# Layer 0's border between attention output and feed-forward: one output chunk and one feed-forward chunk by token halves in place of two each

## What is computed

```python
h = h + g1_l * y_l                                  # y_l = o @ w_o
h = h + g2_l * swiglu_ffn(ada_norm(h, norm_ffn[i], sh2_l, sc2_l), ffn_w_in[i], ffn_w_out[i])
# hc, the context, the same with g1_c, sh2_c, sc2_c, g2_c

def rms_norm(x, g):
    y = x * lax.rsqrt(jnp.mean(x * x, axis=-1, keepdims=True) + EPS)
    return y * g

def ada_norm(x, g, shift, scale):
    return rms_norm(x, g) * (1.0 + scale) + shift

def swiglu_ffn(h, w_in, w_out):
    a, g = jnp.split(h @ w_in, 2, axis=-1)
    return (jax.nn.silu(a) * g) @ w_out
```

## Time and profile before

| | us |
|---|---|
| three runs | 1509.53, 1512.20, 1512.33 |
| median | 1512.2 |
| the profiled execution | 1508.97 |
| its span in the trace | 1507.7 |
| PE busy | 1488.3 (99%) |
| DVE busy | 1079.9 (72%) |
| ACT busy | 718.2 (48%) |

### The profile page before, as it was taken

How to read it: one execution, slowest core, us unless ns; L and a number is a source line. 1 busy time by engine, 2 the same in 40 slices (tenths; PEclk the granted TensorE clock), 3 DMA queues, 4 the chain that set the end, 5 groups by cost and what they waited for, 6 DMA issues and landing times.

```text
span 1507.7 us, 21700 instructions
## 1 busy us (share of the span) xinstructions
PE 1488.3 (99%) x8915; PEld 1259.4 (84%) x8915; DVE 1079.9 (72%) x1496; ACT 718.2 (48%) x1020; POOL 77.4 (5%) x104
## 2 busy tenths in 40 slices
PE   7999999999999999999999999999999999999998
PEld 6878767988888888899678888899888888988887
DVE  6664685687857686577977667579789856779973
ACT  5422585342222312346765555545566546566553
POOL 0210141000000000000000000033000000000000
PEclk9999999999999999999999999999999999999999
DMA  9865424145455462223155555656565555565652
GB/s 361 299 197 180 115 42 168 57 149 186 153 183 167 140 203 84 93 94 121 50 193 171 193 191 192 205 176 215 178 194 174 197 189 169 172 204 174 196 189 84
DMA packets 243250, 252.44 MB, mean 167 GB/s; under 512 B 17757, under 2 KB 234176, under 8 KB 243152
## 3 DMA queue, kind: packets, MB, share of 16 engines
q1 hardware_dynamic: 241600, 248.53, 50.6%
q0 software_dynamic: 944, 1.87, 0.3%
q10 hardware_dynamic: 608, 0.66, 0.1%
...
## 4 chain that ended last, share of the span: by engine, by line
PE 92%; DVE 4%; ACT 2%; issue 1%; DMA 1%; SPq 0%; DVEq 0%; ACTq 0%
PE psum L437 89%; PE psum L1170 3%; DVE wl L423 2%; ACT scr L1211 1%; DMA vtok<-in_ctx 1%; ACT wh L416 0%; PE psum L1141 0%; DVE hT L2440 0%; DVE xl L753 0%; DVE scr L745 0%; DVE scr L2386 0%; DVE kl L1898 0%; DVE mix L2400 0%; ACT scr L839 0%; DVE sums L1281 0%
## 5 line engine op out<-in xcount | busy, mean ns | idle before, releaser
L423 DVE TENSOR_TENSOR wl<-raw,wh 128x2048 fp32r<-128x2048 f32 (+1 forms) x183 | 413.3, 2260 | 144.1 <-ACT wh L416 143.9
L416 ACT ACTIVATE wh<-raw 128x2048 fp32r<-128x2048 f32 (+1 forms) x183 | 344.3, 1883 | 282.2 <-PE psum L437 277.9
L437 PE MATMUL psum<-x,wh 128*128 128x512 f32 (+1 forms) x1520 | 461.3, 364 | 0.0
L437 PE MATMUL psum<-x,wl 128*128 128x256 f32 x1312 | 367.3, 280 | 0.0
L437 PEld LDWEIGHTS psum<-x,wh 128*128 128x128 f32 x1520 | 271.7, 188 | 48.2 <-issue 0.8
L437 PE MATMUL psum<-xh,wh 128*128 128x512 f32 (+1 forms) x704 | 254.1, 361 | 2.2 <-DVE xl L753 1.9
L437 PE MATMUL psum<-xl,wh 128*128 128x512 f32 (+1 forms) x704 | 250.2, 355 | 0.0
L437 PE MATMUL psum<-xh,wl 128*128 128x512 f32 (+1 forms) x704 | 250.1, 355 | 0.0
L437 PEld LDWEIGHTS psum<-x,wl 128*128 128x128 f32 x1312 | 248.2, 189 | 0.0
L437 PEld LDWEIGHTS psum<-xh,wh 128*128 128x128 f32 x704 | 132.8, 189 | 25.2 <-issue 4.6
L437 PEld LDWEIGHTS psum<-xh,wl 128*128 128x128 f32 x704 | 132.9, 189 | 19.0
...
## 6 DMA issues: line engine op xcount, KB each, us to landing
raw<-in_ffn_w_in SPq DMA_DIRECT2D x44, 1024.0 KB, 5.0
pairs<-in_ada_w SPq DMA_DIRECT2D x22, 1024.0 KB, 7.2
raw<-in_w_ffn_gate SPq DMA_DIRECT2D x22, 1024.0 KB, 5.2
raw<-in_w_ffn_up SPq DMA_DIRECT2D x22, 1024.0 KB, 5.1
raw<-in_w_ffn_down SPq DMA_DIRECT2D x19, 1024.0 KB, 4.9
pre<-in_ada_w SPq DMA_DIRECT2D x16, 1024.0 KB, 9.7
raw<-in_ffn_w_out SPq DMA_DIRECT2D x16, 1024.0 KB, 4.9
raw<-in_na_w_qkv SPq DMA_DIRECT2D x10, 1024.0 KB, 7.3
```

Source lines behind the costliest of these rows:

```text
L416: act.e.activation(wh[:, c % NSPL, 0:z], raw[:, p % NRAW, 0:z], ACT.Copy).then_inc(W.hi, 1)
L423: dve.e.tensor_tensor(wl[:, c % NSPL, 0:z], raw[:, p % NRAW, 0:z], wh[:, c % NSPL, 0:z].bitcast(F32), ALU.subtract).then_inc(W.lo, 1)
L437: return pe.e.matmul(o, l, r, start=start, stop=stop, skip_group_check=shared)
```

## The change

O3 and F2 are taken whole; O4 and F1 stay in halves.

PE: O1, O2, O3 whole; O4 half 0; O4 half 1 with the sum column of token half 0 at step 6 and the spread at step 10; F1 half 0, k by k, with sum column and spread of token half 1 at its steps 10 and 14; F1 half 1, k by k; F2 whole; F3 whole. DVE and ACT: O3 has whole residuals, squares and sums, so that only two half squares and two half sums are left for each token half (argument `first=6`). F2's split moves from `ffn0_act` and `ffn0_dve` ahead of O4's first residual, into `o0_act` and `o0_dve`. In the first half's norm DVE has O4's half 1 residual after k = 2 and its two half sums after k = 4, and ACT its two half squares after k = 3. The other edits are semaphore counts and the banks that F2's output is read from.

```diff
-            for step in st_o0[:2]:
+            for step in st_o0[:3]:
...
-                group_T([x[:, :] for x in bank[2 * i:2 * i + 2]], [where[step]], xh1, xl1, TT, lambda k: pe.wait_ge(A0.o_lo, 2 * k + 2), k_outer=i == 0)
-            third, fourth = where["o0", 2], where["o0", 3]
-            pe.wait_ge(O0.res, 4)
-            half_T(bank[0], third, xh1, xl1, 0, nothing).then_inc(X.tile, 1)
+                b = bank[0:2] if i % 2 == 0 else bank[2:4]
+                if i == 2:
+                    pe.wait_ge(O0.res, 4)
+                group_T([x[:, :] for x in b], [where[step]], xh1, xl1, TT, lambda k: pe.wait_ge(A0.o_lo, 2 * k + 2), k_outer=i == 0)
+            fourth = where["o0", 3]
             pe.wait_ge(O0.res, 8)
             half_T(bank[2], fourth, xh1, xl1, 0, nothing).then_inc(X.tile, 1)
-            half_T(bank[1], third, xh1, xl1, 1, nothing, between=norm_steps_pe(1, 0, 7, 8, 11)).then_inc(W.used, 1)
-            half_T(bank[3], fourth, xh1, xl1, 1, nothing).then_inc(W.used, 1)
+            half_T(bank[3], fourth, xh1, xl1, 1, nothing, between=norm_steps_pe(1, 0, 7, 6, 10)).then_inc(W.used, 1)
...
+        def half_squares_act(s, res, summed, first=4):
+
+            w, n = slice(s * T, s * T + T), KT - first
+            for j in range(n):
+                act.wait_ge(O0.res, res + 2 * first + n * s + j + 1)
                 act.wait_ge(O0.sum, summed + 1)
-                act.e.activation(scr[:, (3 + j) % 6, w], hT[:, 4 + j, w], ACT.Square).then_inc(O0.square, 1)
...
-            for step in st_o0[:3]:
+            for step in st_o0:
                 split_for(split_hi, where[step])
                 if step[1] >= 1:
...
-            half_squares_act(0, 0, 0)
+            half_squares_act(0, 0, 0, 6)
...
-            for step in st_o0[:2]:
+            for step in st_o0[:3]:
...
+                if i == 2:
+                    sums_dve(1, 0, 0)
                 dve.wait_ge(W.used, c + 1)
-                residual_dve(i, bank[2 * i:2 * i + 2], 0, 2, 0)
+                residual_dve(i, bank[0:2] if i % 2 == 0 else bank[2:4], 0, 2, 0)
                 if i == 1:
                     sums_dve(0, 0, 0)
-            split_for(split_lo, where["o0", 2])
-            sums_dve(1, 0, 0)
-            for i in (2, 3):
-                dve.wait_ge(X.tile, KT + 3 + i - 1)
-                half_residual_dve(i, 0, bank[2 * i - 4], 0, 2, 0)
-            half_sums_dve(0, 0, 0)
+            split_for(split_lo, where["o0", 3])
+            sums_dve(2, 0, 0)
+            dve.wait_ge(X.tile, KT + 4)
+            half_residual_dve(3, 0, bank[2], 0, 2, 0)
+            half_sums_dve(0, 0, 0, 6)
             half_recip_dve(1, 0)
...
-            c0, c1 = (where[step] for step in st_ffn0[0][0][:2])
+            c0 = where[st_ffn0[0][0][0]]
             pe.wait_ge(O0.res, 12)
-            half_T(bank[0], c0, xh2, xl2, 0, lambda k: pe.wait_ge(N.xl, 16 + k + 1), k_outer=True)
-            half_T(bank[2], c1, xh2, xl2, 0, nothing, between=norm_steps_pe(1, 1, 11, 5, 11))
+            half_T(bank[0], c0, xh2, xl2, 0, lambda k: pe.wait_ge(N.xl, 16 + k + 1), k_outer=True, between=norm_steps_pe(1, 1, 9, 10, 14))
+            half_T(bank[1], c0, xh2, xl2, 1, lambda k: pe.wait_ge(N.xl, 24 + k + 1), k_outer=True).then_inc(W.used, 1)
             pe.wait_ge(O0.res, 16)
-            half_T(bank[1], c0, xh2, xl2, 1, lambda k: pe.wait_ge(N.xl, 24 + k + 1), k_outer=True).then_inc(W.used, 1)
-            half_T(bank[3], c1, xh2, xl2, 1, nothing).then_inc(W.used, 1)
...
-                for step in (up[2:] if third == 0 else up) + (dn if third < 2 else []):
+                for step in (up[1:] if third == 0 else up) + (dn if third < 2 else []):
...
             for k in range(KT):
                 half_normed_act(1, 0, 0, 1, xh2, k)
-            split_hi(where["o0", 3] + AHEAD)
-            half_squares_act(1, 0, 0)
+                if k == 3:
+                    half_squares_act(1, 0, 0, 6)
             half_root_act(1, 1)
...
             for k in range(KT):
                 half_normed_dve(1, 0, 0, 1, xh2, xl2, k)
-                if k == 4:
-                    dve.wait_ge(W.used, where["o0", 2] + 1)
-                    half_residual_dve(2, 1, bank[1], 0, 2, 0)
+                if k == 2:
+                    dve.wait_ge(W.used, where["o0", 3] + 1)
+                    half_residual_dve(3, 1, bank[3], 0, 2, 0)
+                elif k == 4:
+                    half_sums_dve(1, 0, 0, 6)
             half_low_dve(1, 0, 0, 1, xh2, xl2, KT - 1)
-            dve.wait_ge(W.used, where["o0", 3] + 1)
-            half_residual_dve(3, 1, bank[3], 0, 2, 0)
-            split_lo(where["o0", 3] + AHEAD)
-            half_sums_dve(1, 0, 0)
             half_recip_dve(1, 1)
...
-                        dve.e.scalar_tensor_tensor(two(s), two(s), 0.5, up_out(p, g, 2, m), ALU.mult, ALU.mult).then_inc(G0.g2, 1)
+                        dve.e.scalar_tensor_tensor(two(s), two(s), 0.5, two(g[m]), ALU.mult, ALU.mult).then_inc(G0.g2, 1)
```

More of the change, by code:

```diff
@@ L1445, in sums_dve, with half_sums_dve @@
                     dve.e.tensor_tensor(acc[:, :], acc[:, :], scr[:, (k - 1) % 6, :], ALU.add).then_inc(O0.sum, 1)
[L1447 to L1451, removed]
+        def half_squares_act(s, res, summed, first=4):
+            w, n = slice(s * T, s * T + T), KT - first
+            for j in range(n):
+                act.wait_ge(O0.res, res + 2 * first + n * s + j + 1)
                 act.wait_ge(O0.sum, summed + 1)
-                act.e.activation(scr[:, (3 + j) % 6, w], hT[:, 4 + j, w], ACT.Square).then_inc(O0.square, 1)
[L1455 to L1460, removed]
+                act.e.activation(scr[:, (first + j - 1) % 6, w], hT[:, first + j, w], ACT.Square).then_inc(O0.square, 1)
+        def half_sums_dve(s, square, summed, first=4):
+            w, n = slice(s * T, s * T + T), KT - first
+            for j in range(n):
+                dve.wait_ge(O0.square, square + first + n * s + j + 1)
+                dve.wait_ge(O0.sum, summed + first - 1 + n * s + j)
+                dve.e.tensor_tensor(acc[:, w], acc[:, w], scr[:, (first + j - 1) % 6, w], ALU.add).then_inc(O0.sum, 1)
         def half_residual_dve(i, s, b, l, j, base):
@@ L1527, in ffn0_banks_pe, with up_out @@
             return [x[:, :] for x in b]
-        def up_out(p, b, first, m):
-            return two(b[m]) if p else both_halves(first, m)
+        def up_out(p, b, m):
+            return two(b[m]) if p else both_halves(0, m)
         def up_halves_pe():
-            c0, c1 = (where[step] for step in st_ffn0[0][0][:2])
+            c0 = where[st_ffn0[0][0][0]]
             pe.wait_ge(O0.res, 12)
-            half_T(bank[0], c0, xh2, xl2, 0, lambda k: pe.wait_ge(N.xl, 16 + k + 1), k_outer=True)
-            half_T(bank[2], c1, xh2, xl2, 0, nothing, between=norm_steps_pe(1, 1, 11, 5, 11))
+            half_T(bank[0], c0, xh2, xl2, 0, lambda k: pe.wait_ge(N.xl, 16 + k + 1), k_outer=True, between=norm_steps_pe(1, 1, 9, 10, 14))
+            half_T(bank[1], c0, xh2, xl2, 1, lambda k: pe.wait_ge(N.xl, 24 + k + 1), k_outer=True).then_inc(W.used, 1)
             pe.wait_ge(O0.res, 16)
-            half_T(bank[1], c0, xh2, xl2, 1, lambda k: pe.wait_ge(N.xl, 24 + k + 1), k_outer=True).then_inc(W.used, 1)
-            half_T(bank[3], c1, xh2, xl2, 1, nothing).then_inc(W.used, 1)
         def down_halves_pe():
@@ L1552, in down_halves_pe @@
             half_T(last_banks[3][0], last_dn[3], ah0, al0, 0, nothing).then_inc(X.tile, 1)
-            half_T(last_banks[2][1], last_dn[2], ah0, al0, 1, nothing, between=norm_steps_pe(2, 0, 18, 8, 11)).then_inc(W.used, 1)
+            half_T(last_banks[2][1], last_dn[2], ah0, al0, 1, nothing, between=norm_steps_pe(2, 0, 16, 8, 11)).then_inc(W.used, 1)
             half_T(last_banks[3][1], last_dn[3], ah0, al0, 1, nothing).then_inc(W.used, 1)
@@ L1596, in ffn0_act @@
                             act.wait_ge(G0.lo, 2 * (p - 3) + m + 1)
-                        act.e.activation(two(scr[:, (2 * p + m) % 6, :]), up_out(p, a, 0, m), ACT.Tanh, scale=0.5).then_inc(G0.tanh, 1)
+                        act.e.activation(two(scr[:, (2 * p + m) % 6, :]), up_out(p, a, m), ACT.Tanh, scale=0.5).then_inc(G0.tanh, 1)
                     for m in range(2):
@@ L1652, in ffn0_dve @@
                         dve.wait_ge(G0.tanh, 2 * p + m + 1 if p else 2)
-                        dve.e.scalar_tensor_tensor(two(s), two(s), 1.0, up_out(p, a, 0, m), ALU.add, ALU.mult).then_inc(G0.g1, 1)
+                        dve.e.scalar_tensor_tensor(two(s), two(s), 1.0, up_out(p, a, m), ALU.add, ALU.mult).then_inc(G0.g1, 1)
                     for m in range(2):
@@ L1670, in ffn0_dve @@
                     if third == 2 and i == 1:
[L1671 removed]
+                        sums_dve(0, 10, 9)
             split_for(split_lo, last_dn[2])
[L1673 removed]
+            sums_dve(1, 10, 9)
             for i in (2, 3):
[L1675 removed]
+                dve.wait_ge(X.tile, KT + 3 + 1 + i - 1)
```

(3 more changed lines are left out.)

10 lines of the change are left out of this document (3 added, 7 removed).

## The result

| | before | after |
|---|---|---|
| median of 21 runs each, us | 1512.36 | 1514.77 |
| lowest and highest | 1509.40, 1513.87 | 1513.14, 1516.52 |
| the profiled execution's span | 1507.7 | 1513.7 |
| first matmul of O3 to first of F3 | 48.16 | 49.57 |

The ratio of the runs is 1.0018, with a 95% interval of 1.0012 to 1.0023: 2.7 us slower, 1.8 to 3.5. The forecast was 1513.4, 1.2 us above before.

The account below looks back on a forecast made before the run. TensorE (PE), 92% of the chain, was taken to bound the kernel: -1.17 us of matmuls and +2.41 between them make +1.24, so 1512.2 + 1.2 = 1513.4 us, range 1509.8 to 1516.2.

Parts of the forecast that it names:

- the forecast's own range: Whole kernel: 1512.9 to 1514.5 us around 1513.4, the main case, given 70%.
- The forecast's bounds: O3 to F3: from uncertain low-part waits and slots of the moved sums, +0.8 to +2.3 us in the stretch.
- Fewer matmuls: O3 and F2 on PE: whole chunks at 10.93 us where halves take 11.52, -1.17 us together.
- The chain: From t0, O4's second half starting on PE, to F1's second half: less cover, waits 0.65, 0.97, 1.20 us.
- O4's residual on DVE: Behind O3: F2's moved split and the sums finish before O4's residual is wanted, 0.15 us to spare.
- The rival that the gain stands: O3 to F3: the chain keeps ahead of PE, stretch 46.5 us, -1.7, total 1510.5; 8%.
- The rival of the clock: At the new waits: PE drops to 1.2 GHz, 10.93 us more per chunk, total 1516 to 1524; 3%.
- The step that failed: Whole kernel: the stretch's +1.2 us is added to the median of 1512.2, giving 1513.4.
- it is taken up later: Behind the border: a later PE wait set by a transfer absorbs the 1.2 us, total 1512.2; 7%.
- The base: Whole kernel: forecast counted from the runs' median, 3.2 us above the profiled execution of 1508.97.

Follow-up runs that it names:

- e5: Against before: O3 whole, F2 in halves, O4's second residual, squares and sums behind the first half's norm; O3 to F3 47.12 us, ratio 0.9997.
- e2: Against before: F2 taken whole, O3, O4 and F1 left in halves; O3 to F3 51.55 us, ratio 1.0025.
- e6: Against the changed kernel: O4's second residual, squares and sums behind the first half's norm; O3 to F3 52.54 us, ratio 1.0046.
- e7: The kernel before, unchanged, for a second trace; O3 to F3 48.17 us, span 1509.3 us.
- e4: The changed kernel again, for a second trace, against before; O3 to F3 49.59 us, ratio 1.0016.
- e11: The changed kernel a third time, against before; O3 to F3 49.60 us, ratio 1.0008.

## Why the prediction was right or wrong

- *Sign and size.* Slower, within 0.2%, in the outer range of 1509.8 to 1516.2: all three came so. But 1514.77 lies outside the forecast's own range (1512.9 to 1514.5), and the outer range held by the 1.5 us to either side that it left for the spread of the runs. The size was half of what was measured (1.2 against 2.7, 1.8 to 3.5), and the missing part is not in the border. The forecast's bounds do not follow from their terms either: 1.24 less 0.2 and 0.4, or plus 0.8, is +0.6 to +2.0 us and not +0.8 to +2.3; the measured 1.41 lies within both.
- *Fewer matmuls, -1.17 us.* Right. In after F2 takes 10.91 us (303.70 to 314.61) and O3 10.88 (265.04 to 275.92), against 11.52 for a chunk in halves. e5 shows one such saving bare: 47.12 us with one chunk whole and PE busy in all of it.
- *The chain.* Sum column +2.18 (forecast 2.20), spread +4.17 (4.00), gaps 0.62, 0.84 and 1.07 (0.65, 0.97, 1.20), second half from 297.43, t0 + 15.76 (15.61), its length 6.27 (6.17), stretch 49.57 (49.40). The spread was late because the column cost 0.47 and not 0.36, and 0.08 more went at the seam behind it. Before has both costs, 0.46 for the first token half's column (279.55 to 280.01) and 0.36 for the second's, and the forecast took the second for both. The gaps were a little short because PE went on 0.53 after a low part's start, the lower end of the 0.52 to 0.63 that were seen.
- *O4's residual on DVE, 0.15 us to spare.* Right, and nearly used up: DVE's sums run from 280.33 for 1.48 us, and the residual follows at 281.87, 0.20 after t0 as wanted.
- *The rival that the gain stands* is out for this kernel. Its mechanism was right all the same where half a chunk more lies between (e5).
- *The rival of the clock* was right as a mechanism and wrong in its place. Waits of 0.6 to 1.1 us did not bring the level down: 1.00 over the whole stretch in after. Some 4 us of near standstill did, by 1.1 and 2.1 us (e2, e6), and the old wait of 1.75 us does in some executions. The forecast took the trace of before, where it had not fallen, for the rule; e7, the same kernel, has the fall. Its price was too high: 10.93 us for a chunk is a doubling of the step, and e6 has 0.213 us in place of 0.120 for 256 columns, for 7 us at most.
- *The step that failed* is the one that makes the time of the whole kernel out of the stretch alone: nothing behind the border was given a price, with the reason, under "it is taken up later", that the later waits "move along". They do not merely move along: in attention 1 the changed kernel takes 0.67 us more, by a pause that no row of before shows, and a fall of the clock adds 0.55 or 2.1 in the traces that have it, before's second one (e7, 2.1) among them. 1.41 + 0.67 = 2.1 us agrees with the lower groups of e4 and e11 (2.1 and 2.0) and lies within 1.8 to 3.5; the remaining 0.6 of the 2.7 is not settled. No row of before could have shown the pause, and its cause stays open.
- *The base.* The forecast stood on the median, 1512.2, and the profile on 1508.97. The profile of before lies in the lower group of its runs. The 3.2 us between them is close to the 3.3 of the one stage's pitch; no run of before's upper group was traced to show it.
